# Two-layer transformer on one core: further expert blocks in pairs, pair adds on GpSimd, silu between the halves of the next weights

## Chip, cores, metric

One Trainium2 chip, one of its cores. The metric is the time of one execution on the device in microseconds. The kernel is one program that computes two transformer blocks; it is timed as a whole.

## What is computed

The first block is a mixer (differential attention and a state-space branch) and a mixture-of-experts feed-forward network; the second is a stack of two layers with banded and forgetting attention and a convolutional feed-forward network. All arithmetic is in float32. The change lies in the mixture of experts and in what follows it at once. There are 512 tokens of 1024 features; each goes to 8 of 64 experts with a hidden width of 256.

```python
def expert_block(args):            # one block: up to 128 rows of one expert
    tok_b, w_b, e = args
    xb = h[tok_b]
    hid = jax.nn.silu(xb @ w_e_gate[e]) * (xb @ w_e_up[e])
    return (hid @ w_e_down[e]) * w_b[:, None]

routed = segment_sum(out, buf_tok)           # 8 rows of each token added
shared = (silu(h @ w_sh_gate) * (h @ w_sh_up)) @ w_sh_down
f = routed + shared
x = x + gt2 * rmsnorm(f, g_post_ffn)         # then the next block's rms_norm(x)
```

An expert that has more than 128 tokens needs further blocks.

## The kernel before

**Engines and order.** The function `experts` runs one instruction list on each engine: SyncE (`sp`) asks for the weights, GpSimd (`pool`) gathers token rows from DRAM and scatters results with indirect DMAs, TensorE (`pe`) multiplies, ScalarE (`act`) and VectorE (`dve`) do the rest. Each engine works its list strictly in the order in which it is written; engines wait for each other by semaphores only.

**Main blocks.** The 64 main blocks, one per expert, are unrolled (`for n in range(N + 1)`, lines 3232, 3344 and 3507). Float32 products are made of three faster ones: each matrix is split in a rounded high part (ScalarE, a copy to `F32R`) and a low part (VectorE, value minus high part), and `three` multiplies high by high, high by low and low by high. For block n, ScalarE rounds the gate half and the up half of the weights (`round_gate_up`, L3303, two instructions of 128x2048), VectorE makes their low parts (`part_gate_up`, L3394). TensorE waits for both low parts (`gu_parted`, 2n + 2) and issues 24 matmuls (3 for each of 8 slices, each over 512 columns that hold gate and up together). Then ScalarE makes the silu (L3353) and VectorE the product with the up part (L3518), TensorE turns it (`turn_hid`, L3165), ScalarE and VectorE split it, and the 12 down matmuls follow one block later. TensorE's list per block is: gate and up of n, turn the gathered rows of n + 2 (`turn_x`, L3160), down of n - 1, turn hid of n. ScalarE's: split hid of n - 1, round gate and up of n + 1, silu of n, round down of n (L3309), round x of n + 2, evict y of n - 1 (L3362). VectorE's runs likewise. Weights lie in three sets of buffers (`SETS = 3`); those of block n are asked for when the gate and up matmuls of block n - 3 are done.

**Further blocks.** A loop with a trip count from the data (`Fori(0, n, 1)`, lines 3066, 3130, 3271, 3374, 3534) takes blocks beyond the 64, one after the other, with one set of buffers and plain float32 matmuls. In a round TensorE does gate and up, turns hid, does down, and turns the next gathered rows. The first weights are asked for after the up and the down matmuls of main block 61.

**Combine.** `combine_norm` loads the 8 expert rows of each token, tile by tile (4 tiles of 128 tokens), in two halves of 4 rows. TensorE sums the first half and the shared expert's output in PSUM (`add`), VectorE adds the second half in two steps (`half`, L3654 over 2048 elements and L3655 over 1024), then both (`total`, L3660). Square and root (ScalarE, GpSimd), scaling and residual (`finish`, L3664 and L3665), and the weighing of the row for the next norm (`weigh`, L652) follow, then TensorE turns the row and ScalarE and VectorE split it (`high_out`, `low_out`). ScalarE and VectorE also split the first weights of the next stage ahead of time (`high_ahead`, `low_ahead`, L253).

Of the kernel before, what the change touches and what calls it, by code (L numbers as in the profile page):

```python
# [11 lines left out]
P = 128  # L12
# [146 lines left out]
class SplitRing:  # L159
# [63 lines left out]
    def low_ahead(self, c, dve):  # L223
        self.low(c, dve)
        self.low_made = True
# [2658 lines left out]
def experts(c, s, h_dram, table, y_dram, acc, early):  # L2884
# [48 lines left out]
    nrow = carve([TABLE], parts=1)  # L2933
# [52 lines left out]
    fetch = c.sb(s, "fetch_rows", [P, 4], I32)  # L2986
    give = c.sb(s, "give_rows", [P, 4], I32)
# [21 lines left out]
    l_gu_in, l_down_in, l_fetch_in, l_give_in = (c.sem(f"later_{n}") for n in ("gate_up_in", "down_in", "fetch_in", "give_in"))  # L3009
    l_gathered, l_scattered = c.sem("later_gathered"), c.sem("later_scattered")  # L3010
    l_up_done, l_silud, l_gated, l_turned, l_copied, l_down_done = (c.sem(f"later_{n}") for n in ("up_done", "silued", "gated", "hid_turned", "hid_copied", "down_done"))
    l_x_turned, l_x_left, l_x_right, l_y_ready = (c.sem(f"later_{n}") for n in ("x_turned", "x_left", "x_right", "y_ready"))
    passed = c.sem("waits_passed")
    with ExitStack() as sb:
        block = sb.enter_context(nc.Block())

        def trips(eng):
            return eng.value_load(count[0:1, 0:1], min_val=1, max_val=MOST_LATER)

        lset = N % SETS  # L3020

        @block.sync
        def _(sp):
# [10 lines left out]
            def later_gate_up(e):  # L3034
                for v, w in enumerate((gate_w, up_w)):
                    sp.dma_start(gu[lset][:, v], w[bass.ds(e, 1)].rearrange("o (p k) n -> p (o k) n", p=P)).then_inc(l_gu_in, 16)

            def later_down(e):
                sp.dma_start(wd[lset], down_w[bass.ds(e, 1)].rearrange("o (k p) n -> p (o k) n", p=P)).then_inc(l_down_in, 16)

            def weights(b):
                return sp.value_load(erow[0:1, bass.ds(b, 1)], min_val=0, max_val=EXPERTS - 1)
# [18 lines left out]
            sp.wait_ge(up_done, N - SETS + 1)  # L3061
            sp.sem_inc(l_up_done, 1)
            sp.wait_ge(down_done, N - SETS + 1)
            sp.sem_inc(l_down_done, 1)
# [9 lines left out]
            sp.wait_ge(l_gu_in, 32 * n)  # L3074
            sp.sem_inc(passed, 1)
            sp.wait_ge(l_down_in, 16 * n)
            sp.sem_inc(passed, 1)

        @block.gpsimd
        def _(pool):  # L3080
# [12 lines left out]
            def later_gather():  # L3093
                nc.gpsimd.indirect_dma_start(xg[0][:], None, h_dram, bass.IndirectOffsetOnAxis(fetch[:, 0:1], 0),
                                             bounds_check=SEQ - 1, oob_is_err=False).then_inc(l_gathered, 16)
# [15 lines left out]
            rows(fetch, l_fetch_in, N)  # L3111
            rows(give, l_scattered, N)
            for j in range(N + 3):
# [4 lines left out]
                elif j == N - 2:  # L3118
                    pool.wait_ge(x_turned, j + 1)
                    pool.wait_ge(gathered[0], 16 * (j // 2 + 1))  # L3120
                    pool.wait_ge(l_fetch_in, 16)
                    later_gather()
                if j >= 3:
                    scatter(j - 3)
            pool.wait_ge(gathered[1], 16 * (N // 2))
            pool.wait_ge(l_gathered, 16)
            rows(fetch, l_fetch_in, N + 1)
            pool.wait_ge(listed, 1)
            n = trips(pool)
            with pool.Fori(0, n, 1) as i:  # L3130
                pool.wait_ge(l_fetch_in, 16 * i + 32)
                pool.wait_ge(l_x_turned, i + 1)
                pool.sem_inc(passed, 1)
                later_gather()
                pool.wait_ge(l_scattered, 16 * i + 16)
                rows(give, l_give_in, i + N)
                pool.wait_ge(l_give_in, 16 * i + 16)
                pool.wait_ge(l_y_ready, i + 2)
                pool.sem_inc(passed, 1)
                nc.gpsimd.indirect_dma_start(y_dram, bass.IndirectOffsetOnAxis(give[:, 2:3], 0), y[0][:], None,  # L3140
                                             bounds_check=SEQ * TOP_K - 1, oob_is_err=False).then_inc(l_scattered, 16)
                pool.wait_ge(l_gathered, 16 * i + 32)
                rows(fetch, l_fetch_in, i + (N + 2))
            for p in range(2):
                pool.wait_ge(scattered[p], 16 * (N // 2))
            pool.wait_ge(l_scattered, 16 * n + 16)
            pool.wait_ge(l_gathered, 16 * n + 16)
            pool.wait_ge(l_fetch_in, 16 * n + 32)
# [3 lines left out]
        def _(pe):  # L3152
# [110 lines left out]
            pe.wait_ge(l_gathered, 16)  # L3263
            turn_x(0).then_inc(l_x_turned, 1)
# [3 lines left out]
            pe.sem_inc(l_turned, 1)  # L3268
            pe.wait_ge(listed, 1)
            n = trips(pe)  # L3270
            with pe.Fori(0, n, 1) as i:
                pe.wait_ge(l_x_left, i + 1)
                pe.wait_ge(l_x_right, i + 1)
                pe.wait_ge(l_gu_in, 32 * i + 32)
# [18 lines left out]
        def _(act):  # L3293
# [455 lines left out]
```

## Time and profile before

| | us |
|---|---|
| median of 3 runs | 3199.24 (3198.63 to 3200.02) |
| the profiled execution's own time | 3197.57 |
| its span | 3195.9 |
| TensorE matmuls busy | 2930.6 (92% of the span) |
| VectorE busy | 1774.6 (56%) |
| ScalarE busy | 1414.9 (44%) |
| GpSimd busy | 533.1 (17%) |
| main expert blocks | about 1115 to 1750 |
| further blocks | about 1751 to 1790 |
| combine | 1796 to 1866 |

The span runs from the first to the last instruction; the time also has what lies around it. All times within the kernel are counted from the start of the span. Busy time of an engine is the time in which its instructions ran, waiting left out. A line of the timeline gives start and duration, then engine, source line, operation, what is written and what is read; in square brackets how long the engine stood idle before it, and what ended that.

### The profile page before, as it was taken

Reading aid. Unit: us, or ns where it says so; the run is one execution under the profiler, and the core shown is the slowest. Engines: PE = TensorE matmul, PEld = TensorE weight load, DVE = VectorE, ACT = ScalarE, POOL = GpSimd, SP = SyncE. Lnnn points to the kernel's source line nnn. Section 1 sums busy time; section 2 is a strip of 40 time slices with the busy share of each in tenths; the row PEclk is TensorE's granted clock in tenths of the full one; section 3 lists DMA queues with packets and bytes.
Section 4 is the critical chain, followed back from the end, with each engine's and each line's share of the span. In section 5 each row is a group of like instructions: output and inputs, shape, how many; then the busy total and the mean of one; then the engine's idle time right before and its main releaser. Section 6 shows DMA issues by size and latency. Waiting matters only on the chain. (4 is left out here: it accounts for less than half of the span.)

```text
span 3195.9 us, 36485 instructions
## 1 busy us (share of the span) xinstructions
PE 2930.6 (92%) x14410; PEld 2346.5 (73%) x14410; DVE 1774.6 (56%) x2033; ACT 1414.9 (44%) x1832; POOL 533.1 (17%) x702
## 2 busy tenths in 40 slices
PE   7978899898998799999999679889999998889998
PEld 4856788787886387777777358678887797678887
DVE  4447745436544498888887253455544327455543
ACT  3324525336223188888787123433323225333322
POOL 0005514124101522222222100000000104000000
PEclk9989999998999799999999889999999999999999
DMA  5210101022652399999997632123332301223331
GB/s 199 60 55 1 56 32 54 27 54 73 211 191 92 114 338 365 364 370 370 373 373 304 261 113 93 53 81 92 105 105 66 96 27 54 73 80 93 93 105 40
DMA packets 276890, 455.94 MB, mean 143 GB/s; under 512 B 24400, under 2 KB 206288, under 8 KB 257648
## 3 DMA queue, kind: packets, MB, share of 16 engines
q1 hardware_dynamic: 250560, 398.82, 36.0%
q0 software_dynamic: 26160, 54.79, 4.8%
q8 instruction: 115, 1.88, 0.3%
q14 instruction: 55, 0.45, 0.0%
HBM read 450.63 MB, written 39.08 MB: 153 GB/s over the span
## 5 line engine op out<-in xcount | busy, mean ns | idle before, releaser
L253 DVE TENSOR_TENSOR weight_part<-weights,weight_part 128x2048 fp32r<-128x2048 f32 (+1 forms) x65 | 148.1, 2279 | 161.2 <-ACT weight_part L242 161.2
L1037 ACT ACTIVATE up_room<-banks,tap_columns 128x512 f32<-128x512 f32 x88 | 68.6, 779 | 314.0 <-PE banks L298 314.0
L293 PE MATMUL banks<-hT_r,weight_part 128*128 128x512 f32 x496 | 200.9, 405 | 4.6 <-PEq L878 2.9
L242 ACT ACTIVATE weight_part<-weights 128x2048 fp32r<-128x2048 f32 (+1 forms) x65 | 121.7, 1872 | 175.8 <-PE banks L293 169.9
L1078 DVE SCALAR_TENSOR_TENSOR up_room<-banks,tap_columns,up_room 128x511 f32<-128x511 f32 x88 | 65.9, 749 | 238.7 <-ACT up_room L1037 238.7
L298 PE MATMUL banks<-hT_r,weight_part 128*128 128x512 f32 x496 | 196.3, 396 | 0.0
L703 POOL TENSOR_SCALAR branch_mean<-branch_mean 128x1 f32<-128x1 f32 x20 | 4.4, 222 | 1113.2 <-ACT up_room L697 747.3
L293 PE MATMUL banks<-hT_r,weight_part_o 128*128 128x512 f32 x432 | 174.3, 403 | 7.1 <-PEq L110 4.2
L253 DVE TENSOR_TENSOR weight_part_o<-weights,weight_part_o 128x2048 fp32r<-128x2048 f32 (+2 forms) x49 | 106.9, 2181 | 129.5 <-ACT weight_part_o L242 129.5
L298 PE MATMUL banks<-hT_r,weight_part_o 128*128 128x512 f32 x432 | 170.5, 395 | 0.0
L297 PE MATMUL banks<-h_low,weight_part 128*128 128x512 f32 x432 | 169.7, 393 | 0.0
L297 PE MATMUL banks<-h_low,weight_part_o 128*128 128x512 f32 x432 | 169.2, 392 | 0.0
L3085 POOL DMA_INDIRECT gathered<-h_tokens,block_rows x64 | 113.0, 1765 | 225.0 <-PE banks L3160 205.2
L3155 PE MATMUL banks<-weights_r,gatheredT_r 128*128 128x512 f32 x336 | 131.9, 393 | 0.0
L242 ACT ACTIVATE weight_part_o<-weights 128x2048 fp32r<-128x2048 f32 (+2 forms) x49 | 89.4, 1824 | 95.9 <-PE banks L293 91.3
L293 PEld LDWEIGHTS banks<-hT_r,weight_part 128*128 128x128 f32 x496 | 94.7, 191 | 26.7 <-issue 7.2
L2623 DVE TENSOR_REDUCE minus_maxima<-banks 128x2 f32<-128x1536 f32 x32 | 56.2, 1757 | 97.8 <-PE banks L2532 97.8
L298 PEld LDWEIGHTS banks<-hT_r,weight_part 128*128 128x128 f32 x496 | 94.1, 190 | 22.2
L3090 POOL DMA_INDIRECT expert_rows<-lent,block_rows x64 | 64.5, 1008 | 244.2 <-ACT lent L3362 234.7
L3154 PE MATMUL banks<-gate_up_high,gatheredT_r 128*128 128x512 f32 x256 | 104.3, 407 | 0.0
L3154 PE MATMUL banks<-h_tokens_r,gatheredT_r 128*128 128x512 f32 x256 | 103.0, 403 | 0.0
L3394 DVE TENSOR_TENSOR weights_r<-weights,h_tokens_r 128x2048 fp32r<-128x2048 f32 x42 | 95.5, 2292 | 12.2 <-ACT h_tokens_r L3303 11.8
(704 smaller groups left out, 8746.3 us busy)
## 6 DMA issues: line engine op xcount, KB each, us to landing
weights<-in_w_e_gate SPq DMA_DIRECT2D x44, 1024.0 KB, 16.0
weights<-in_w_e_up SPq DMA_DIRECT2D x44, 1024.0 KB, 18.6
hT<-in_w_e_down SPq DMA_DIRECT2D x44, 1024.0 KB, 18.9
weights<-in_w_up SPq DMA_DIRECT2D x88, 512.0 KB, 5.1
gate_up<-in_w_e_gate SPq DMA_DIRECT2D x22, 1024.0 KB, 15.4
gate_up<-in_w_e_up SPq DMA_DIRECT2D x22, 1024.0 KB, 18.4
down<-in_w_e_down SPq DMA_DIRECT2D x22, 1024.0 KB, 18.8
weights<-in_w_down SPq DMA_DIRECT2D x20, 1024.0 KB, 5.0
```

Of the source, the lines that this page charges most:

```text
L242: c.nc.scalar.activation(self.parts[n % 2][0][:, 0:z], self.raw[n % RAW_SLOTS][:, 0:z], ACT.Copy).then_inc(self.high_ready, 1)
L253: c.nc.vector.tensor_tensor(low[:, 0:z], self.raw[n % RAW_SLOTS][:, 0:z], high[:, 0:z].bitcast(F32), ALU.subtract).then_inc(self.low_ready, 1)
L293: ins = c.nc.tensor.matmul(out, lhs[0], rhs[0], start=start, stop=False)
L297: c.nc.tensor.matmul(out, lhs[0], rhs[1], start=False, stop=False)
L298: return c.nc.tensor.matmul(out, lhs[1], rhs[0], start=False, stop=stop)
L1037: nc.scalar.activation(a[:, f % 2, v], c.ps[:, 2 * (f % 4) + v], ACT.Identity, scale=conv[:, 2, ch:ch + 1], bias=bias[:, ch:ch + 1]).then_ ...
L1078: nc.vector.scalar_tensor_tensor(a[:, f % 2, v, 1:], c.ps[:, 2 * (f % 4) + v, 0:SEQ - 1], conv[:, 1, ch:ch + 1], a[:, f % 2, v, 1:], ALU.m ...
L3085: nc.gpsimd.indirect_dma_start(xg[n % 2][:], None, h_dram, bass.IndirectOffsetOnAxis(tab[:, n, 0:1], 0), bounds_check=SEQ - 1, oob_is_err= ...
L3090: nc.gpsimd.indirect_dma_start(y_dram, bass.IndirectOffsetOnAxis(tab[:, n, 2:3], 0), y[n % 2][:], None, bounds_check=SEQ * TOP_K - 1, oob_ ...
L3154: nc.tensor.matmul(out, lhs[0], rhs[0], start=start, stop=False)
L3155: nc.tensor.matmul(out, lhs[0], rhs[1], start=False, stop=False)
L3394: nc.vector.tensor_tensor(gu_low[i][:, v], gu[i][:, v], gu_high[n % 2][:, v].bitcast(F32), ALU.subtract).then_inc(gu_parted, 1)
```

## The change

In the main blocks silu and its product move between the two halves of the next block's rounding and low parts. The further blocks run two at a time, each with buffers and semaphores of its own; an odd count is rounded up, and the count is at least two. Their weights are asked for as soon as the set is free. In the combine, GpSimd does the first of the two adds of `half` for tiles 0 to 2 and the low part of the first weights, and `finish` and `weigh` stand earlier in the lists.

```diff
 # ScalarE, main blocks
                 if n + 1 < N:
-                    round_gate_up(n + 1)
+                    round_half(n + 1, 0)
                 if n < N:
                     act.wait_ge(up_done, n + 1)
+                    if N - SETS <= n < N - 1:
+                        act.sem_inc(l_up_done[n - N + SETS], 2)
                     ...
                     nc.scalar.activation(sl[n % 2][:], c.ps[:, n % 2, 0:EF], ACT.Silu).then_inc(silud, 1)
+                    if n + 1 < N:
+                        round_half(n + 1, 1)
                     round_down(n)
 # VectorE, main blocks
                 if n + 1 < N:
-                    part_gate_up(n + 1)
+                    part_half(n + 1, 0)
                 if n < N:
                     dve.wait_ge(silud, n + 1)
                     ...
                     nc.vector.tensor_tensor(hid[n % 2][:], sl[n % 2][:], c.ps[:, n % 2, EF:2 * EF], ALU.mult).then_inc(gated, 1)
+                    if n + 1 < N:
+                        part_half(n + 1, 1)
                     dve.wait_ge(d_rounded, n + 1)
 # SyncE, further blocks
-            with sp.Fori(0, n, 1) as i:
-                e = weights(i)
-                sp.wait_ge(l_up_done, i + 1)
-                later_gate_up(e)
-                sp.wait_ge(l_down_done, i + 1)
-                later_down(e)
+            with sp.Fori(0, n, 2) as i:
+                e = [weights(p, i + p) for p in range(2)]
+                for p in range(2):
+                    sp.wait_ge(l_up_done[p], i + 2)
+                    sp.sem_inc(passed, 1)
+                    later_gate_up(p, e[p])
+                for p in range(2):
+                    sp.wait_ge(l_down_done[p], i + 2)
+                    sp.sem_inc(passed, 1)
+                    later_down(p, e[p])
 # TensorE, further blocks (up(p, ks): gate and up matmuls; down(p): down matmuls)
+                def down(p):
+                    pe.wait_ge(l_copied[p], i + 4)
+                    pe.wait_ge(l_down_in[p], 8 * i + 16)
+                    pe.wait_ge(l_y_ready[1 - p], i + 2 + 2 * p)
+                    ...
+                        up(0, range(KD)).then_inc(l_up_done[0], 2)
+                up(1, range(0, 4))
+                pe.wait_ge(l_gated[0], i + 4)
+                pe.wait_ge(l_copied[1], i + 2)
+                turn_hid(0).then_inc(l_turned[0], 2)
+                up(1, range(4, KD)).then_inc(l_up_done[1], 2)
+                down(0)
+                pe.wait_ge(l_gated[1], i + 4)
+                pe.wait_ge(l_copied[0], i + 4)
+                turn_hid(1).then_inc(l_turned[1], 2)
+                down(1)
+                for p in range(2):
+                    pe.wait_ge(l_gathered[p], 8 * i + 32)
+                    pe.wait_ge(l_x_left[1 - p], i + 2 + 2 * p)
+                    pe.wait_ge(l_x_right[1 - p], i + 2 + 2 * p)
+                    turn_x(p).then_inc(l_x_turned[p], 2)
 # GpSimd: four row fetches instead of two ahead of the main blocks; loop over pairs likewise
-            rows(fetch, l_fetch_in, N)
-            rows(give, l_scattered, N)
+            for p in range(2):
+                rows(fetch[p], l_fetch_in[p], N + p)
+                rows(give[p], l_scattered[p], N + p)
 # VectorE, routing: the count
-            L(V.tensor_scalar(nrow[:, 2:3], nrow[:, 0:1], 1.0, None, ALU.max))
+            L(V.tensor_scalar(even[:, 0:TABLE // 2], iota[0:1, 0:TABLE:2], nrow[:, 0:1], None, ALU.is_lt))
+            L(V.tensor_reduce(nrow[:, 1:2], even[:, 0:TABLE // 2], AX, ALU.add))
+            L(V.tensor_scalar(nrow[:, 2:3], nrow[:, 1:2], 1.0, 2.0, ALU.max, ALU.mult))
 # Combine, ScalarE
             square(1)
+            turn.high_out(c, act, 0)
             square_x(1)
             square(2)
-            turn.high_out(c, act, 0)
+            turn.high_out(c, act, 1)
             square_x(2)
             square(3)
-            turn.high_out(c, act, 1)
             c.split.high_ahead(c, act)
+            turn.high_out(c, act, 2)
             square_x(3)
-            turn.high_out(c, act, 2)
             turn.high_out(c, act, 3)
 # Combine, GpSimd
-            for t in range(NT):
-                root(t)
-                rows.root(c, pool, t)
+            def pairs(t):
+                r = got[:, (2 * t + 1) % 4]
+                pool.wait_ge(landed[(2 * t + 1) % 4], 16 * (t // 2 + 1))
+                nc.gpsimd.tensor_tensor(r[:, 0:2], r[:, 0:2], r[:, 2:4], ALU.add).then_inc(paired, 1)
+
+            pairs(0)
+            root(0)
+            pairs(1)
+            rows.root(c, pool, 0)
+            root(1)
+            pairs(2)
+            rows.root(c, pool, 1)
+            root(2)
+            rows.root(c, pool, 2)
+            root(3)
+            rows.root(c, pool, 3)
+            c.split.low_ahead_on(c, pool)
 # Combine, VectorE (half(t) waits for the pair add, and adds both itself for tile 3 alone)
             half(0)
             total(0)
+            finish(0)
             half(1)
-            finish(0)
             total(1)
-            half(2)
             weigh(0)
             finish(1)
+            half(2)
             total(2)
             turn.low_out(c, dve, 0)
-            half(3)
             weigh(1)
             finish(2)
+            half(3)
             total(3)
             turn.low_out(c, dve, 1)
             weigh(2)
             finish(3)
             turn.low_out(c, dve, 2)
-            c.split.low_ahead(c, dve)
             weigh(3)
             turn.low_out(c, dve, 3)
```

## Rows read from the trace of the kernel before

**Rows 1.** Busy time by stretch: us, busy of each engine (records), clock, DMA share, GB/s.
```profile
1120.00:1740.00 620.00, 596.04 (x2870) 482.14 (x2870) 539.44 (x377) 505.22 (x437) 171.90 (x123) 1.00 0.94 362
1740.00:1796.00 56.00, 38.03 (x118) 20.51 (x116) 6.84 (x11) 9.14 (x12) 9.51 (x12) 0.91 0.37 135
```
**Rows 2.** Timeline of TensorE: last gate and up matmul of blocks 0 and 63.
```profile
1120.99 0.40 PE L3156 MATMUL banks<-gate_up_high,lent_r 128*128 128x512 f32 x1
...
1743.20 0.39 PE L3156 MATMUL banks<-h_tokens_r,lent_r 128*128 128x512 f32 x1
```
**Rows 3.** Timelines of TensorE, ScalarE and VectorE, blocks 59 and 60.
```profile
1697.86 0.48 PE L3154 MATMUL banks<-h_tokens_r,gatheredT_r 128*128 128x512 f32 x1
...
1703.22 0.39 PE L3156 MATMUL banks<-h_tokens_r,lent_r 128*128 128x512 f32 x1
...
1709.06 0.48 PE L3154 MATMUL banks<-gate_up_high,gatheredT_r 128*128 128x512 f32 x1
...
1714.50 0.39 PE L3156 MATMUL banks<-gate_up_high,lent_r 128*128 128x512 f32 x1
...
1704.23 1.92 ACT L3303 ACTIVATE gate_up_high<-gate_up 128x2048 fp32r<-128x2048 f32 x1 [0.93 <-DMA gate_up<-in_w_e_up]
1706.05 0.36 ACT L3353 ACTIVATE lent<-banks 128x256 f32<-128x256 f32 x1
...
1706.18 2.29 DVE L3394 TENSOR_TENSOR gate_up_r<-gate_up,gate_up_high 128x2048 fp32r<-128x2048 f32 x1 [0.55 <-ACT gate_up_high L3303]
1708.39 0.41 DVE L3518 TENSOR_TENSOR lent<-lent,banks 128x256 f32<-128x256 f32 x1
```
**Rows 4.** Timelines of ScalarE, VectorE and TensorE behind the last main block.
```profile
1743.63 0.38 ACT L3353 ACTIVATE lent<-banks 128x256 f32<-128x256 f32 x1 [4.75 <-PE banks L3156]
1743.91 1.90 ACT L3309 ACTIVATE shared_gated_r<-down 128x2048 fp32r<-128x2048 f32 x1
...
1748.06 0.42 DVE L3511 TENSOR_TENSOR lent_r<-banks,hiddenT_r 128x256 fp32r<-128x256 f32 x1
...
1748.53 0.50 PE L3154 MATMUL banks<-shared_gated_r,hiddenT_r 128*128 128x512 f32 x1 [1.94 <-DVE lent_r L3511]
```
**Rows 5.** Line 2962, loads of gate and up weights: issue to landing.
```profile
DMA to landing us min/median/max: 4.8/16.6/21.1
```
**Rows 6.** Timelines of TensorE and ScalarE, the two further blocks.
```profile
1754.45 5.80 PE L3277 MATMUL banks<-weights,gatheredT 128*128 128x512 f32 x9 [1.98 <-issue]
1759.65 3.60 PE L3277 MATMUL banks<-weights,gatheredT 128*128 128x512 f32 x8
...
1765.41 3.67 PE L3287 MATMUL banks<-hT,hiddenT 128*128 128x512 f32 x8 [0.70 <-DVE hiddenT L3540]
1768.92 1.04 PE L3160 MATMUL banks<-ident,gathered 128*128 128x128 f32 x8
...
1769.26 1.11 ACT L3381 ACTIVATE lent<-banks,give_rows 128x1024 f32<-128x1024 f32 x1 [5.50 <-PE banks L3287]
...
1786.95 1.11 ACT L3381 ACTIVATE lent<-banks,give_rows 128x1024 f32<-128x1024 f32 x1 [5.50 <-PE banks L3287]
```
**Rows 7.** Timeline of VectorE in the combine.
```profile
1829.39 2.29 DVE L3654 TENSOR_TENSOR expert_rows<-expert_rows 128x2048 f32<-128x2048 f32 x1 [2.65 <-DMA expert_rows<-expert_rows]
...
1860.68 1.27 DVE L652 SCALAR_TENSOR_TENSOR x_gained<-x_tok,rstd,norm_rows 128x1024 f32<-128x1024 f32 x1
```
**Rows 8.** Timelines of GpSimd and VectorE where both have work, earlier stages.
```profile
440.80 1.83 POOL L2406 TENSOR_TENSOR kT_r<-kT,x_tok_r 128x768 fp32r<-128x768 f32 x1
...
440.83 2.36 DVE L614 TENSOR_TENSOR kT<-gate_rows,rope 128x512 f32<-128x512 f32 x1
443.22 0.69 DVE L616 TENSOR_TENSOR kT<-kT,gate_rows 128x512 f32<-128x512 f32 x1
...
578.80 0.45 POOL L2496 TENSOR_TENSOR oT_low_r<-oT_low,oT_r 128x128 fp32r<-128x128 f32 x1
...
578.86 0.47 DVE L2618 TENSOR_SCALAR gate_rows<-gate_rows,sum_squares 128x128 f32<-128x128 f32 x1 [3.22 <-POOL sum_squares L2492]
```

More of the change, by code:

```diff
@@ L224, in low_ahead, with low_ahead_on @@
         self.low(c, dve)
+        self.low_made = True
+    def low_ahead_on(self, c, pool):
+        n = self.lows
+        self.lows += 1
+        pool.wait_ge(self.high_ready, n + 1)
+        z = self.sizes[n]
+        high, low = self.parts[n % 2]
+        c.nc.gpsimd.tensor_tensor(low[:, 0:z], self.raw[n % RAW_SLOTS][:, 0:z], high[:, 0:z].bitcast(F32), ALU.subtract).then_inc(self.low_ready, 1)
         self.low_made = True
@@ L2932, in experts @@
     desti = carve([NT, TOP_K], I32)
-    nrow = carve([TABLE], parts=1)
+    nrow, even = carve([TABLE], parts=1), carve([TABLE], parts=1)
     at = used[0]
@@ L2985, in experts @@
     tab = c.sb(s, "block_rows", [P, N, 4], I32)
-    fetch = c.sb(s, "fetch_rows", [P, 4], I32)
-    give = c.sb(s, "give_rows", [P, 4], I32)
+    fetch = two("fetch_rows", [P, 4], I32)
+    give = two("give_rows", [P, 4], I32)
     xg = two("gathered", [P, D])
@@ L3017, in trips @@
         def trips(eng):
-            return eng.value_load(count[0:1, 0:1], min_val=1, max_val=MOST_LATER)
-        lset = N % SETS
+            return eng.value_load(count[0:1, 0:1], min_val=2, max_val=MOST_LATER)
+        lset = [(N + p) % SETS for p in range(2)]
         @block.sync
@@ L3124, in _ @@
                     scatter(j - 3)
-            pool.wait_ge(gathered[1], 16 * (N // 2))
-            pool.wait_ge(l_gathered, 16)
-            rows(fetch, l_fetch_in, N + 1)
+            for p in range(2):
+                pool.wait_ge(l_gathered[p], 16)
+                rows(fetch[p], l_fetch_in[p], N + 2 + p)
             pool.wait_ge(listed, 1)
             n = trips(pool)
[L3130 to L3143, printed above, removed]
+            with pool.Fori(0, n, 2) as i:
+                for p in range(2):
+                    pool.wait_ge(l_fetch_in[p], 8 * i + 32)
+                    pool.wait_ge(l_x_turned[p], i + 2)
+                    pool.sem_inc(passed, 1)
+                    later_gather(p)
+                for p in range(2):
+                    pool.wait_ge(l_scattered[p], 8 * i + 16)
+                    rows(give[p], l_give_in[p], i + (N + p))
+                for p in range(2):
+                    pool.wait_ge(l_give_in[p], 8 * i + 16)
+                    pool.wait_ge(l_y_ready[p], i + 4)
+                    pool.sem_inc(passed, 1)
+                    nc.gpsimd.indirect_dma_start(y_dram, bass.IndirectOffsetOnAxis(give[p][:, 2:3], 0), y[p][:], None,
+                                                 bounds_check=SEQ * TOP_K - 1, oob_is_err=False).then_inc(l_scattered[p], 16)
+                    if p == 0:
+                        for q in range(2):
+                            pool.wait_ge(l_gathered[q], 8 * i + 32)
+                            rows(fetch[q], l_fetch_in[q], i + (N + 4 + q))
@@ L3262, in _ @@
             pe.wait_ge(x_parted, N)
-            pe.wait_ge(l_gathered, 16)
-            turn_x(0).then_inc(l_x_turned, 1)
+            for p in range(2):
+                pe.wait_ge(l_gathered[p], 16)
+                if p:
+                    pe.wait_ge(l_x_left[0], 2)
+                    pe.wait_ge(l_x_right[0], 2)
+                turn_x(p).then_inc(l_x_turned[p], 2)
             pe.wait_ge(gated, N)
@@ L3331, in _ @@
                     nc.scalar.activation(by_row[:, tile, b * 64:(b + 1) * 64], c.ps[:, TURNED_AT[tile] + b].rearrange("p (q r) -> p q r", r=KD), ACT.Copy).then_inc(copied, 1)
-            round_gate_up(0)
+            for v in range(2):
+                round_half(0, v)
             for f in range(2):
```

188 lines of the change are left out of this document (98 added, 90 removed).

## Prediction

> **What bounds the kernel now.** I read the table by slices first, then stretches of it, then the timeline of single blocks, the later blocks and the combine. The change touches one stretch, from 1,100 to 1,866 us; it adds nothing ahead of it that lies on a path, and behind it the same work follows, only sooner or later. So the question is how long three stages in it take.
>
> In the stage of the 64 main blocks [rows 1] four things are nearly full at once: TensorE is busy 596 of 620 us at the full clock, VectorE 539, ScalarE 505, and the DMA engines 94% of the time. The question is which of them sets the time of a block. The last gate and up matmul of block 0 starts at 1120.99 and that of block 63 at 1743.20 [rows 2]: 622.2 us for 63 steps, 9.88 us each. Call that moment of block n U(n).
>
> Block 59 shows what ends last [rows 3]. U(59) is 1703.22. The up half of block 60's weights lands a little late; ScalarE rounds it from 1704.23, and VectorE takes its low part from 1706.18 (1.95 us after the rounding began, 2.29 us long). The silu of block 59 stands in ScalarE's queue behind that rounding and starts at 1706.05, the product stands in VectorE's queue behind the low part and starts at 1708.39, TensorE can turn the product only then and starts block 60 at 1709.06: 5.84 us after U(59). Where the weights are in time the same step is about 4.0 us, all of it TensorE's own work (turning a gathered block, the down matmuls, turning hid). So a block costs 9.4 us where weights are early, up to 11 where they are late, 9.88 in the mean: transfers pace it, but TensorE's queue is only half a microsecond below.
>
> **The change in the main blocks.** It puts silu(n) ahead of the rounding of the second half of block n+1's weights, and the product ahead of that half's low part. No instruction is added. What it removes is the wait just seen, product and turning behind the late half. What it adds is a new dependence: both engines take their queues in order, so the second half of block n+1 cannot be rounded before silu(n), silu(n) not before U(n), and every gate and up matmul of block n+1 (they take both halves at once, line 3240, behind the wait on two more low parts) not before that half is done. Before, rounding and low part of block n+1 ran under the matmuls of block n. The cycle from U(n) to U(n+1), each link from a row:
> - U(n) to silu: 0.43 us (1743.20 to 1743.63) [rows 2, 4].
> - silu to the next ScalarE instruction when that one's data are there: 0.28 (1743.63 to 1743.91) [rows 4].
> - start of a rounding to start of its low part: 1.95 [rows 3].
> - low part 2.29 [rows 3], and 0.05 from VectorE's end to TensorE's start (1748.06 + 0.42 = 1748.48, start at 1748.53) [rows 4]: 2.34.
> - first to last of the 24 matmuls: 5.36 in block 59, 5.44 in block 60 [rows 3]; 5.40.
>
> The sum is 10.40 us. TensorE's own work between (about 4.0 of the 5.0 us from U(n) to the next start) hides in it. It is a floor for every one of the 63 steps, where before the mean was 9.88: 655.2 - 622.2 = **33.0 us lost**. Nothing else lengthens the cycle by my count. VectorE needs about 8.5 us and ScalarE about 8.2 of it. The weights of block n+2 are asked for at U(n-1) and take 16.6 us in the median, 21.1 at most [rows 5]; their second half is wanted only two cycles and 0.7 us after that, at 21.5, so even the slowest is in time, and 9.88 us worth of transfers fit into 10.40. Late transfers, which cost now, are then absorbed. If the steps of silu and rounding overlapped more than I see, 10.3 would give 27 us; if late weights came on top in the busiest blocks, 10.5 would give 39.
>
> **The further blocks.** There are two of them in this run (two rounds of the loop in the trace). Before, one took 17.69 us, from one eviction to the next (1769.26 to 1786.95) [rows 6], and TensorE idles while silu, product and copy of the same block pass. In its parts: gate and up, 16 records from 1754.45 to 1763.25, 8.80 us, since the clock is low at first (0.91 granted in the mean of the stretch [rows 1]); at the full clock a record takes 0.44 (the down matmuls: (3.67 - 0.59)/7), so 7.04. Down begins at 1765.41, and its eviction 3.85 later, 1.11 long. After, counted from the start of the first gate and up matmul: up(0) 8.80; up(1) 7.04 with the turning of hid(0), 0.4, between its halves, which hides silu and product of block 0; then down(0) from 16.2, its eviction from 20.1 to 21.2; down(1) waits for that eviction (same banks) and runs from 21.2, its eviction starts at 25.1. Before, the second eviction started 1786.95 - 1754.45 = 32.5 after. That is 7.4 saved. In front of it stands a second turning of gathered rows, 1.04 us [rows 6], which waits for the copy of the first (0.8): 1.9 lost. Weights of both are asked for at U(61) and U(62) and are there. Net **5.5 us gained**; the bounds are 3 (a stall when the second down starts, or a slower loop entry with more registers) and 8 (all clock back).
>
> **The combine.** Here VectorE's queue sets the time: it is full from tile 1 on, and the last weighing starts at 1860.68 [rows 7]. The change takes three adds of 2.29 us [rows 7] and the low part of the first weights, 2.28 for the same length, off VectorE and puts them on GpSimd, and moves finish and weighing forward. GpSimd's own adds: 1.83 us for 768 elements [rows 8]; by length 4.9 for 2048, a little less with a fixed part, so 4.75. If the engines ran side by side, VectorE would be rid of the adds of tiles 1 and 2 and of the low part: 2.29 + 2.29 + 2.28 = 6.9, some 7 us gained. The add of tile 0 gives nothing: GpSimd takes 2.5 us longer for it than VectorE did, most of which the wait for TensorE's sum of that tile hides.
>
> But they don't. GpSimd's subtract at 440.80 runs 1.83 us, and VectorE's add of 512 elements, which starts 0.03 later and has two operands in SBUF, takes 2.36 us instead of 0.69 [rows 8]: it stood until GpSimd was through. The 0.69 is L616's just behind it, of the same size and kind, when GpSimd is through. Now the places. The second rows of tile 2 land at 1829.39 [rows 7], a few tenths from the time at which the root of tile 1 lets finish(1) start (total of tile 1 near 1827, square and root 2.2 to 2.4 more): finish has two operands in SBUF, so it or its second half waits for the whole 4.75 us, which is 4.65 on the path to half(2). The low part on GpSimd follows the last root in its queue; the last weighing waits for that same root. Both get free together, and a GpSimd instruction that follows its own root starts first: 578.80 against VectorE's 578.86 behind the same root [rows 8]. So the weighing waits 4.65 more. 7 - 4.65 - 4.65 = -2.3, less about 0.8 that is won back in VectorE's idle time behind the first: **1.5 us lost** instead of 7 gained. Bounds: 7 gained when nothing collides, 6 lost when the small roots also wait each time behind VectorE's adds.
>
> The Trainium skill, page "SBUF — State Buffer", section "SBUF: two separate sides", says that VectorE and GpSimd share a port pair as an exclusive lock, taken for a whole instruction by a VectorE instruction with two SBUF inputs; by that rule, too, the combine gains nothing, and the trace agrees (2.36 us instead of 0.69). Its page "GPSIMD Engine Reference", section 3.1, gives 4.497 us for such an add of 2048 elements; the sum by it would be 0.8 us lower; no row of this kernel shows that size on GpSimd.
>
> Three more edits cost nothing. Two small VectorE instructions ahead of the block count (some 0.2 us each) lie in front of 8 us in which VectorE waits for ScalarE. Two more row fetches on GpSimd, 0.6 us each, end before the third gather's wait does. More semaphores are cleared between stages; at most a microsecond.
>
> **Sum.** 33.0 - 5.5 + 1.5 = +29.0 us. The profiled execution took 3197.57, so 3226.6; it lies 1.7 below the median of 3199.24, so **3228 us** in the median, 0.9% slower.
>
> **Rivals.**
> - *Adds run free.* The combine gains 7 instead of losing 1.5: 3219.7. Against it stands the collision in the rows; for it, that my places rest on times within a microsecond, and a different order could dodge one of the two. Chance 0.13.
> - *Transfers go on pacing the blocks, so the reorder costs nothing* (the other side). The DMA engines are 94% busy, and ScalarE's and VectorE's waits in this stage lead back to landings [rows 3]. If the period stayed 9.88, the sum would be 3199.2 - 5.5 + 1.5 = 3195.2. It decides if the cycle of five links is really under 9.9, that is, if rounding and low part of the second half took 0.5 us less than the rows say, or if the order on the queues did not bind. I see no way for either; removing the late product would then help too, some microseconds more. Chance 0.05 within 0.2%, 0.03 beyond it.
> - *The cycle is longer than its floor.* If late weights or a late low part of the down weights push the rounding back, say 10.65 per block, it is 16 us more: 3244. VectorE's last instruction before the next product ends only some 0.1 us ahead of it. Chance 0.07.
> - The forecast itself: 0.72.
>
> **Numbers.** About 0.2% (6.4 us) is what a measurement of this kernel can tell from none. Slower holds forecast, free adds and long cycle: 0.92. Same 0.05, faster 0.03. The range takes in 27 to 39 for the blocks and the combine's bounds, not the ends together: 3216 to 3238.
>
> **What the profile after would show.** Distances from U(n) to U(n+1) nearly constant at 10.4; TensorE idle some 0.7 us before each block, ended by VectorE's L3394 line, not by the product; ScalarE's waits for weights nearly gone and the DMA share down to about 0.9; product about 0.85 us after U(n) in all blocks. One pass of about 25 us from first gate and up matmul to last eviction. In the combine the adds on GpSimd 4.5 to 4.9 us, a finish instruction of some 5.9 us, and a last weighing of about 6. I am wrong if the distance is under 10.2, or if the last weighing is short.

## Result and the profile after

The changed kernel takes 3233.56 us in the median, against 3199.63 for the kernel before beside it: ratio 1.0102, 95% interval 1.0087 to 1.0116, 1% slower. The forecast was 3228 in 3216 to 3238. Its own executions scatter more than usual, 3225.78 to 3235.34; the profiled one is the fastest (span 3224.1, against 3195.9). A second measurement of the unaltered kernel (below) has its ratio at 1.0107 and a profiled span of 3232.0. One of the four executions of the reorder alone (10278 us) and one of the eleven of the pairs alone (11563 us), further below, took over three times as long as the rest and are left out of the medians given there.

I follow both traces by the same moments, with U(n) as in the prediction. "To the loads" runs from U(63) to the issue of the combine's first load, "combine" from there to the end of the last weighing.

| | before | after | after, second trace |
|---|---|---|---|
| U(0) | 1120.99 | 1120.69 | 1121.86 |
| U(0) to U(63) | 622.2 | 660.1 | 660.1 |
| to the loads | 52.39 | 45.00 | 45.02 |
| combine | 66.36 | 66.83 | 66.86 |
| all behind it | 1333.9 | 1331.5 | 1338.2 |
| span | 3195.9 | 3224.1 | 3232.0 |

The 28.2 us of the first pair of spans are +37.9 - 7.4 + 0.5, less 0.3 ahead and 2.4 behind. In the second trace the three changed stages agree to 0.03 us; the 8 us between the two lie ahead of block 0 (1.2) and behind the combine (6.7), in stages whose code is the same.

By stretches (columns as in [rows 1], whose lines these answer), the changed kernel:

```profile
1120.00:1779.00 659.00, 606.47 (x2875) 488.36 (x2874) 537.19 (x376) 499.47 (x438) 126.19 (x124) 0.99 0.91 346
1779.00:1832.00 53.00, 35.15 (x120) 20.27 (x118) 7.51 (x11) 9.86 (x13) 9.53 (x12) 0.89 0.30 109
1832.00:1900.00 68.00, 46.95 (x122) 23.73 (x123) 41.76 (x30) 17.36 (x26) 28.45 (x20) 0.81 0.77 296
```

The stage of the main blocks holds the same busy time of VectorE (537 for 539) and ScalarE (499 for 505) in 39 us more, and the DMA share has fallen from 0.94 to 0.91: neither does more, both wait more. TensorE's records add up to 606 us for 596, at nearly the same count (2875 for 2870). Where the engines wait stands in the timelines of TensorE, ScalarE and VectorE from U(59) to U(60), the step of [rows 3]:

```profile
1738.88 0.39 PE L3171 MATMUL banks<-h_tokens_r,lent_r 128*128 128x512 f32 x1
...
1743.92 0.47 PE L3169 MATMUL banks<-gate_up_high,gatheredT_r 128*128 128x512 f32 x1 [0.77 <-issue]
...
1749.30 0.39 PE L3171 MATMUL banks<-gate_up_high,lent_r 128*128 128x512 f32 x1
...
1739.31 0.38 ACT L3392 ACTIVATE lent<-banks 128x256 f32<-128x256 f32 x1 [2.45 <-PE banks L3171]
1739.59 1.91 ACT L3339 ACTIVATE gate_up_high<-gate_up 128x2048 fp32r<-128x2048 f32 x1
...
1739.72 0.42 DVE L3569 TENSOR_TENSOR lent<-lent,banks 128x256 f32<-128x256 f32 x1 [0.47 <-ACT lent L3392]
1741.53 2.29 DVE L3442 TENSOR_TENSOR gate_up_r<-gate_up,gate_up_high 128x2048 fp32r<-128x2048 f32 x1 [1.39 <-ACT gate_up_high L3339]
```

The chain is the one forecast. Silu starts 0.43 behind the last matmul, the rounding 0.28 behind it, the low part 1.94 behind that; it ends at 1743.82, TensorE starts at 1743.92, and its last matmul starts 5.38 later: 10.42 us. The waits say the same for the whole stage (engine, line, what it waited for: us in total, times, longest):

```profile
ACT lent L3392 <- PE banks L3171: 160.0, 63, 6.0
...
PE banks L3169 <- issue: 49.1, 62, 1.7
DVE lent L3569 <- ACT lent L3392: 34.4, 63, 3.0
DVE weights_r L3442 <- ACT h_tokens_r L3339: 29.1, 21, 1.5
DVE weights_r L3442 <- ACT gate_up_high L3339: 29.1, 21, 1.4
```

ScalarE now waits 63 times, once a block, for TensorE, 2.5 us each; no wait of it for weights is left. TensorE waits 62 times, 0.79 us each, and then starts at the end of a low part: the trace puts that down to "issue", because nothing but that semaphore stands in between. The distances from U(n) to U(n+1) are 10.41 at least and 10.43 in the median; the first alone is 12.97.

### The profile page after: what moved, and what is told of

It reads as the page before. It is cut to its first block and busy times, and to the rows that moved or that the text cites. A ratio compares the mean times of both kernels' runs of the same rounds, so it can differ in the third digit from the quotient of the medians.

```text
span 3224.1 us, 36567 instructions
## 1 busy us (share of the span) xinstructions
PE 2937.4 (91%) x14418; PEld 2349.6 (73%) x14418; DVE 1773.8 (55%) x2032; ACT 1409.0 (44%) x1833; POOL 511.3 (16%) x710
## 5 line engine op out<-in xcount | busy, mean ns | idle before, releaser
L3442 DVE TENSOR_TENSOR weights_r<-weights,gate_up_high 128x2048 fp32r<-128x2048 f32 x42 | 96.0, 2287 | 29.1 <-ACT gate_up_high L3339 29.1
L3093 POOL DMA_INDIRECT gathered<-h_tokens,block_rows x64 | 65.2, 1018 | 280.1 <-PE banks L3175 265.6
```

Source lines behind the costliest of these rows:

```text
L3093: nc.gpsimd.indirect_dma_start(xg[n % 2][:], None, h_dram, bass.IndirectOffsetOnAxis(tab[:, n, 0:1], 0), bounds_check=SEQ - 1, oob_is_err= ...
L3442: nc.vector.tensor_tensor(gu_low[i][:, v], gu[i][:, v], gu_high[n % 2][:, v].bitcast(F32), ALU.subtract).then_inc(gu_parted, 1)
```

## The experiments

**The three parts alone, and the whole again.** Only the main blocks' reorder, on the kernel before:

```diff
                 if n + 1 < N:
-                    round_gate_up(n + 1)
+                    round_half(n + 1, 0)
                 ...silu(n)
+                    if n + 1 < N:
+                        round_half(n + 1, 1)
                 # VectorE: part_half(n + 1, 0), product(n), part_half(n + 1, 1) likewise
```


> The kernel before with the reorder in the main blocks alone: silu(n) between the two roundings of block n+1, product between the two low parts. My theory (a cycle of five links, 10.44 us, in every one of the 63 steps): distances between the last gate and up matmuls constant at 10.4 us, main blocks some 35 to 38 us longer, 3235 to 3238 us. The rival (transfers pace the blocks whatever the order): distances spread from 9.4 to 11 with a mean of 9.9, 3200 us.

Measured 3237.83 against 3197.56, ratio 1.0128 (1.0110 to 1.0147). The blocks take 658.2 us, distances 10.38 to 10.52 with 10.44 in the median. One part alone makes the whole loss, and the distance is as good as constant.

Only the further blocks in pairs (the changed kernel with both halves ahead of the silu again and the combine of before):

> The kernel before with the further blocks in pairs, their buffers, semaphores, early loads and the even count, and nothing else. My theory: 7.4 us less between the last main block and the first load of the combine (the trace after shows 45.0 instead of 52.4), so 3192 us, main blocks 622 us as before. The rival (what they gain is given back, since the stage behind starts with a lower clock or its loads come later): 3197 to 3200.

Measured 3193.83 against 3197.56, ratio 0.9988 (0.9979 to 0.9997). Blocks 622.3; to the loads 43.45 instead of 52.39, so 8.9 us gained in this trace. The whole kernel gains less, 3.7 us by the medians and 1.0 to 6.7 by the interval. Part of this is the choice of the trace: with the further blocks untouched the stretch takes 49.6 to 52.4 us in seven traces (mean 51.3), and the kernel before has the longest; with the pairs it takes 43.4 to 45.0 in five (mean 44.1). So the stage gains about 7.2 in the mean. Behind it this trace is 0.4 longer in the combine and 1.9 after it than the kernel before. How much of the gain is given back there in the other executions stays open.

Only the combine:

> The kernel before with the new combine alone (pair adds of tiles 0 to 2 and the low part of the first weights on GpSimd, finish and weighing earlier). My theory (a VectorE instruction with two operands in SBUF stands while GpSimd's instruction runs, twice on the path): the last weighing takes about 5.4 us and ends within 1 us of before, 3199 to 3201 us. The rival (adds beside VectorE's work are free): last weighing 1.3 us, 7 us gained, 3193.

Measured 3198.98, ratio 1.0007 (0.9998 to 1.0016). Its combine takes 66.77 us, 0.4 more than before, which is within the scatter of the old combine (66.0 to 67.4 in seven traces); the last weighing is 5.41 long, as in the changed kernel.

The changed kernel unaltered:

> The changed kernel once more, unaltered. Three of its four executions took 3233 to 3235 us and the profiled one 3226, with a mean granted clock of 0.961 to 0.963 against 0.967. If the difference is in the granted clock of other stages, a second profile near 3233 us shows the main blocks at the same 10.4 us and lower clock in stretches outside the three changed stages; if it is in the changed stages, it shows there.

Measured 3231.93, ratio 1.0107 (1.0091 to 1.0122). In per cent the parts give 1.28 - 0.12 + 0.07 = 1.23, the whole 1.02 and 1.07; the intervals of the terms are wide enough for that.

**Which engine's order costs.** VectorE's product between its low parts, ScalarE's list as before:

```diff
                 # ScalarE: both halves rounded ahead of silu(n), as before
                 # VectorE
                 if n + 1 < N:
-                    part_gate_up(n + 1)
+                    part_half(n + 1, 0)
                 ...product(n)
+                    if n + 1 < N:
+                        part_half(n + 1, 1)
```


> The kernel before with half of the reorder: ScalarE rounds both halves of block n+1 and then makes silu(n), as before; VectorE makes the product between the two low parts. My theory: it is ScalarE's rounding behind the silu that closes the cycle. Without it, from the last gate and up matmul of a block: silu 0.43, product 0.81, low part 1.1 to 3.4, next block possible at 3.5, which is under TensorE's own 4.0; mean distance 9.9, 3199 to 3201 us. The rival (a low part behind the product is enough to lengthen the step): distance 10.1 or more, 3213 us or more.

Measured 3201.67 against 3199.04, ratio 1.0007 (0.9998 to 1.0017); blocks 622.8. The low part behind the product costs nothing while its rounding is not behind the silu.

And a shorter cycle: the same order, but three quarters of the weights are rounded and split ahead of silu and product, one quarter behind:

```diff
+    PIECES = ((0, slice(0, KD)), (1, slice(0, 4)), (1, slice(4, KD)))
-                    round_gate_up(n + 1)
+                    for q in range(2):
+                        round_piece(n + 1, q)
                 ...silu(n)
+                        round_piece(n + 1, 2)
                 # VectorE: part_piece likewise around the product
```


> The reorder with another size: three quarters of block n+1's gate and up weights are rounded and split ahead of silu and product, one quarter (1024 of 4096 columns) behind them. The kernel is otherwise the one before. My theory of five links: 0.43 + 0.28 + 1.0 + 1.2 + 0.05 + 5.4 = 8.4 us, under TensorE's 9.4, so the links bind no more and the distance is back at 9.8 to 9.95; 3198 to 3204 us. The rival (the reorder costs by more instructions or by the late silu itself, not by what stands behind it): over 3225 us.

Measured 3198.34, ratio 1.0000 (0.9990 to 1.0009); blocks 623.8, distances 8.57 to 11.87. With half the work in the rounding and the low part the cycle is some 2 us shorter, falls below the pace of the transfers, and no longer binds. The first step shows it directly, since TensorE has no down matmuls yet to fill it: 8.57 us here, 10.48 with the whole reorder.

The quarter does not gain either, but it removes less than the reorder does. The up half lands in one transfer, and a part of it is still rounded and split ahead of silu and product. ScalarE and VectorE where it landed late:

```profile
1553.62 1.06 ACT L3304 ACTIVATE h_tokens_r<-gate_up 128x1024 fp32r<-128x1024 f32 x1 [0.49 <-DMA gate_up<-in_w_e_up]
1554.58 0.37 ACT L3356 ACTIVATE lent<-banks 128x256 f32<-128x256 f32 x1
...
1553.15 3.43 DVE L3399 TENSOR_TENSOR gate_up_r<-gate_up,h_tokens_r 128x2048 fp32r<-128x2048 f32 x2 [0.24 <-ACT h_tokens_r L3304]
1556.50 0.42 DVE L3525 TENSOR_TENSOR lent<-lent,banks 128x256 f32<-128x256 f32 x1
```

Of the two, only the version with VectorE's order changed takes the product from behind the late half's low part, and its mean distance is still 9.9: that part of the wait was worth nothing. A silu ahead of the late half's rounding was run only with the cycle closed, so what it would be worth without the cycle is not shown.

**What the transfers cost in either order.** 192 KB more per block, copied from the down weights of the block to a buffer in DRAM that nothing reads, on the kernel before and on the reorder alone:

```diff
             for n in range(SETS, N):
                 gate_up(n)
+                sp.dma_start(spare[n], down_w[n][0:48]).then_inc(copied_out, 16)
```


> The kernel before, and with each of main blocks 3 to 63 a copy of 192 KB from DRAM to DRAM that nothing uses: 5 to 10% more transfers per block. If transfers pace its blocks, as I read the trace: distances longer by 0.4 to 0.9 us in the mean, 3225 to 3255 us. If they don't: within 5 us of before.

> The same copies added to the kernel with the reorder in the main blocks alone. My theory (its blocks wait for the cycle of five links at 10.44 us and transfers have 5% to spare): at most 10 us over that kernel, and 3235 to 3248 us, so that it stands within 10 us of the kernel before with the same copies. The rival (transfers and the cycle add): as much over it as the copies cost the kernel before.

In the old order 3225.46, ratio 1.0082 (1.0065 to 1.0098); blocks 646.0 instead of 622.2, distances 7.35 to 13.32. In the new order 3238.49, ratio 1.0121 (1.0104 to 1.0138), for 3237.83 with the reorder without copies. By the medians the same copies cost 26 us in the one order and none that can be told in the other. The traces say where. In the kernel before, 34 of the 63 steps take at most 9.55 us, the pace of TensorE's own work; the others are longer, mostly by late weights. With the copies only 16 are left at that pace. In the new order the blocks take 665.1 us with the copies and 658.2 without: 2.4 of these 6.9 are the first step (below), and 4.5 lie in ten steps of 10.6 to 11.4 us, all in the second half of the stage. So late transfers make the old order longer than TensorE's pace, and the new one has slack for most of them but not for all. That the two would come within 10 us of each other was a miss: they stay 13.0 apart. By stretches, 1120 to 1740 us of both, the old order with copies first:

```profile
1120.00:1740.00 620.00, 578.22 (x2771) 463.74 (x2770) 519.55 (x361) 485.01 (x420) 158.33 (x119) 1.00 0.96 372
```
```profile
1120.00:1740.00 620.00, 566.86 (x2690) 456.12 (x2688) 503.81 (x351) 470.22 (x408) 121.82 (x116) 0.99 0.94 361
```

The DMA share is 0.96 and 0.94, where [rows 1] has 0.94 without copies: in the old order the DMA engines had little room left.

**The collisions in the combine.** Both kernels have the further blocks in pairs and the new combine, the main blocks in the old order. In the first the low part of the first weights goes back to VectorE, behind the last weighing:

```diff
             rows.root(c, pool, 3)
-            c.split.low_ahead_on(c, pool)
             ...
             weigh(3)
+            c.split.low_ahead(c, dve)
             turn.low_out(c, dve, 3)
```


> Pairs of further blocks and the new combine, the main blocks in the order of before; and the low part of the first weights back on VectorE, behind the last weighing, where VectorE waits 1.9 us for the turned row. One of the two collisions is gone. My theory: last weighing 1.3 us instead of 5.4, the low part of 2.3 mostly in that hole, so the combine 3.5 us shorter than with the collision: 3199.5 - 7.4 + 0.5 - 3.5 = 3189. The rival (the weighing isn't what ends the stage): 3192.5.

Measured 3190.3 against 3199.88, ratio 0.9973 (0.9961 to 0.9985). Last weighing 1.28 us, combine 62.57: 4.2 less than with the new combine alone (66.77).

In the second tile 2's pair add is VectorE's as well:

```diff
             root(1)
-            pairs(2)
             rows.root(c, pool, 1)
             # VectorE, half(t): adds the pairs itself
-                if t == NT - 1:
+                if t >= 2:
```


> The same, and the pair add of tile 2 on VectorE too (as for tile 3), so that GpSimd adds only for tiles 0 and 1. Both collisions are gone. My theory: the finish instruction of tile 1 takes 1.2 us instead of 5.4, the add costs VectorE 2.3, so 2 us less than with one collision: 3187 us, the combine 5 us shorter than before. The rival (VectorE's load is what counts): no gain over the kernel with one collision, 3189 to 3191.

Measured 3189.33, ratio 0.9966 (0.9954 to 0.9978); combine 61.08. Its median is the lowest of all, 10.5 us below the kernel before beside it. From the version above it differs by less than the intervals; that the second collision was worth 1.5 us is read from the combine in the two traces. VectorE in its combine:

```profile
1822.76 1.23 DVE L3736 TENSOR_TENSOR x_tok<-x_tok,ffn_out 128x1024 f32<-128x1024 f32 x1
1823.90 2.29 DVE L3723 TENSOR_TENSOR expert_rows<-expert_rows 128x2048 f32<-128x2048 f32 x1
...
1847.24 1.29 DVE L661 SCALAR_TENSOR_TENSOR x_gained<-x_tok,rstd,norm_rows 128x1024 f32<-128x1024 f32 x1 [1.08 <-POOL rstd L645]
1848.44 2.29 DVE L262 TENSOR_TENSOR weight_part<-weights,weight_part 128x2048 fp32r<-128x2048 f32 x1
```

The finish of tile 1 is 1.23 long, though VectorE has one more add of 2.29 behind it, and the low part has moved behind the last weighing.

## Why the prediction was right, point by point

**Main blocks: forecast +33.0, measured +37.9.** The mechanism holds as written: a cycle over silu, rounding, low part and matmuls that was not closed before. Each link came within 0.05 us of its row, and their sum at the end of the stage is 10.42 for 10.40. The mean of the last 62 steps is (660.1 - 12.97)/62 = 10.44, so the floor was 0.04 short, which is 2.4 us over 63 steps. The other 2.5 is a term that I left out, the first step. In it TensorE runs the first 12 of block 1's 24 matmuls at the lower clock (granted 0.50 of full, 1.2 GHz), 0.63 us each where 0.39 is usual. This is the changed kernel's TensorE there:

```profile
1125.78 0.76 PE L3169 MATMUL banks<-h_tokens_r,gatheredT_r 128*128 128x512 f32 x1 [3.32 <-DVE weights_r L3442]
1126.34 0.63 PE L3170 MATMUL banks<-weights_r,gatheredT_r 128*128 128x512 f32 x1
```

Ahead of them it has idled for 3.32 us, because there is no block before block 0 whose down matmuls could fill the time. In the kernel before it idles 0.44 us between these two blocks, and the clock is full. The drop is not certain: with the reorder alone TensorE idled 3.33 us there too, kept the full clock, and the step took 10.48; with the extra copies it fell again (12.92). What decides it stays open. One reading of [rows 1] was a little off, and nothing rested on it: VectorE's and ScalarE's work per block come out as 8.6 and 8.1 us, not 8.5 and 8.2.

**The rival on the other side, transfers pace the blocks anyway, is out**, but its premise was right. Late transfers did make the old order longer than TensorE's own pace (the copies show it), and even so the reorder costs, because its cycle lies above that pace. That removing the late product "would then help too, some microseconds more" has no support: with the product taken from behind the late low part, and the cycle open, the blocks take 622.8 us for 622.2. In [rows 3] the low part itself ends at 1708.47, 0.59 us ahead of TensorE's start, so no more than that was to be had in such a block, by either engine's order. The rival of a longer cycle is out as well: in the changed kernel no step but the first is over 10.53. It takes more transfers than this kernel has to bring it in, as the ten long steps with the copies show.

**Further blocks: forecast -5.5, measured -7.4.** TensorE and ScalarE there:

```profile
1780.77 0.39 PE L3171 MATMUL banks<-h_tokens_r,lent_r 128*128 128x512 f32 x1
...
1794.37 10.54 PE L3294 MATMUL banks<-weights,gatheredT 128*128 128x512 f32 x24 [0.79 <-DVEq L3586]
...
1808.40 3.60 PE L3303 MATMUL banks<-hT,hiddenT 128*128 128x512 f32 x8
...
1813.45 3.67 PE L3303 MATMUL banks<-hT,hiddenT 128*128 128x512 f32 x8 [1.24 <-ACT lent L3429]
...
1801.66 0.38 ACT L3424 ACTIVATE lent<-banks 128x256 f32<-128x256 f32 x1 [7.38 <-PE banks L3294]
...
1812.19 1.11 ACT L3429 ACTIVATE lent<-banks,give_rows 128x1024 f32<-128x1024 f32 x1 [3.16 <-PE banks L3303]
1817.21 1.11 ACT L3429 ACTIVATE lent<-banks,give_rows 128x1024 f32<-128x1024 f32 x1 [3.90 <-PE banks L3303]
```

The order inside is as forecast, the second down waiting 1.24 us for the first eviction. Three sizes were off, and they partly cancel. The start lies 13.60 us behind U(63) instead of 11.25. Of these 2.35 us the second turning, costed at 1.9, has only 0.8: with the pairs but the old order in the main blocks the start lies 12.04 behind U(63), because the 1.98 us in which TensorE idled there [rows 6] take in most of it. The other 1.54 is the clock, which I had not counted: the down matmuls of block 63 take 4.44 us instead of 2.90, at 0.63 each:

```profile
1786.10 0.50 PE L3169 MATMUL banks<-shared_gated_r,hiddenT_r 128*128 128x512 f32 x1 [1.95 <-DVE lent_r L3562]
...
1786.73 0.63 PE L3171 MATMUL banks<-shared_gated_r,lent_r 128*128 128x512 f32 x1
...
1790.54 1.03 PE L3175 MATMUL banks<-ident,gathered 128*128 128x128 f32 x8
```

It is full again at 1790. TensorE idled 1.95 us ahead of them; in the kernel before it idled 1.94 at the same place [rows 4] and kept the full clock. And the last eviction starts 22.84 us behind the start, not 25.1, 2.3 better: I took the first gate and up at its 8.80 us of before, with the clock partly low; here 24 records take 10.54, 0.43 apart, so it is full from the first one. It is tempting to put this down to the shorter idle time ahead of them (0.79 us instead of 1.98), but the other runs speak against it. In four of the seven traces with the further blocks untouched, TensorE idles 1.95 to 1.98 us there as well and the clock is full from the first record, as in the reorder alone:

```profile
1791.53 7.11 PE L3277 MATMUL banks<-weights,gatheredT 128*128 128x512 f32 x16 [1.98 <-issue]
```

So 8.80 is one of two values that the old kernel itself takes, and 7.11 the other. In these four the whole stretch to the loads is 49.6 to 51.3 us instead of 52.39: 1.1 us or more of the gain measured here is the old kernel's own scatter. Net 32.5 - 22.84 - 2.35 = 7.3, and 0.1 between the last eviction and the loads. Without the fallen clock ahead, as in the run of the pairs alone, it is 8.9; against the mean of the seven traces it is 7.2 in the mean of the five with pairs.

**Combine: forecast +1.5, measured +0.5.** Both collisions are there, at the two places named. VectorE and GpSimd:

```profile
1859.51 1.28 DVE L3739 SCALAR_TENSOR_TENSOR ffn_out<-ffn_out,ffn_rstd,gate_rows 128x1024 f32<-128x1024 f32 x1 [0.99 <-POOL ffn_rstd L3700]
1860.83 5.43 DVE L3740 TENSOR_TENSOR x_tok<-x_tok,ffn_out 128x1024 f32<-128x1024 f32 x1
...
1887.19 5.41 DVE L661 SCALAR_TENSOR_TENSOR x_gained<-x_tok,rstd,norm_rows 128x1024 f32<-128x1024 f32 x1 [1.08 <-POOL rstd L645]
...
1850.23 4.51 POOL L3704 TENSOR_TENSOR expert_rows<-expert_rows 128x2048 f32<-128x2048 f32 x1 [2.56 <-DMA expert_rows<-expert_rows]
1854.83 1.26 POOL L643 TENSOR_SCALAR mean_square<-mean_square 128x1 f32<-128x1 f32 x1
...
1859.97 5.20 POOL L3704 TENSOR_TENSOR expert_rows<-expert_rows 128x2048 f32<-128x2048 f32 x1 [0.50 <-DMA expert_rows<-expert_rows]
...
1886.49 0.57 POOL L645 TENSOR_TENSOR rstd<-mean_square,minus_half 128x1 f32<-128x1 f32 x1
1887.02 4.50 POOL L233 TENSOR_TENSOR weight_part<-weights,weight_part 128x2048 fp32r<-128x2048 f32 x1
```

The second half of finish(1), two operands in SBUF, is issued 0.86 us behind GpSimd's add of tile 2 and takes 5.43 us instead of 1.23; it ends at 1866.26, 1.1 us after that add, about one duration of its own. The last weighing is issued 0.17 behind the low part and takes 5.41 instead of 1.28. They cost 4.20 and 4.13 us, where the forecast had 4.65 each: 0.97 less, about the whole difference. For the weighing, GpSimd's instruction took 4.50 us where I took 4.75, and VectorE came 0.17 behind it, not 0.1. For finish(1), VectorE came 0.86 behind, and GpSimd's add took 5.20, its first 0.82 us beside the first half of finish(1) (1859.51 + 1.28 = 1860.79). The +0.5 itself is no more than the scatter of the old combine, 66.0 to 67.4 us in seven traces; that nothing is gained is clear, that 0.5 is lost is not.

The Trainium skill gives 4.497 us for GpSimd's add (page "GPSIMD Engine Reference", section 3.1), and the trace agrees to 0.01 where VectorE is not in its way. The exclusive lock of the Trainium skill (page "SBUF — State Buffer", section "SBUF: two separate sides") is what the two rows of VectorE show. The prediction put the sum by the page's 4.497 at 0.8 us lower; the two waits that it shortens make that 0.5.

The experiments put a price on the collisions: without that of the weighing the combine is 4.2 us shorter, without that of finish(1) 1.5 more. The second is worth so little because VectorE has to make that add itself again, 2.29 us. **The rival that adds run free is out.** The best that was run is 66.36 - 61.08 = 5.3 us shorter, with two adds on GpSimd and the low part behind the last weighing.

**Total.** The terms' sum was +29.0. They measure 37.9 - 7.4 + 0.5 = +31.0, and the medians of the two kernels lie 33.9 apart. The remaining 2.9 are not located: the stages behind the combine, their code unchanged, take 2.4 us less in one trace of the changed kernel and 4.3 more in the other than in the one of before. That 3228 came out near is partly luck: the blocks' 4.9 us too few, and the further blocks' 1.9 and the combine's 1.0 too bad, offset each other.

## What to carry to other kernels

Before an instruction is moved between two halves of another block's work, write down the cycle that it closes: here silu(n) ahead of rounding(n + 1) turned a chain that ran one block ahead into one that starts at each block's last matmul. Add its links from the trace and compare the sum with the pace that something else already sets; above it each block pays the difference, and below it, at the one size tried, the move cost nothing and gained nothing. And give GpSimd long instructions only where VectorE has, for their whole length, nothing with two operands in SBUF on the path, least of all where both wait for the same instruction of GpSimd.

## What the hardware showed that I had not expected

- The collision goes both ways and reaches instructions of one element per partition: 1.26 us at 1854.83 instead of 0.22 for the scaling ahead of the root, which was issued 0.05 behind an add of VectorE with two operands in SBUF. GpSimd's add of tile 2, issued 0.46 us behind the first half of finish(1), took 5.20 instead of 4.51.
- GpSimd's gather instruction became cheaper though no edit touches it. Lines of the groups of GpSimd (busy time, mean ns of one, idle time before it and what ended it), before and then after:

```profile
L3085 POOL DMA_INDIRECT gathered<-h_tokens,block_rows x64 | 113.0, 1765 | 225.0 <-PE banks L3160 205.2 <-issue 14.4 <-DMA block_rows<-block_table 2.7
```
```profile
L3093 POOL DMA_INDIRECT gathered<-h_tokens,block_rows x64 | 65.2, 1018 | 280.1 <-PE banks L3175 265.6 <-issue 11.8 <-DMA block_rows<-block_table 2.7
```

  Its mean is 1018 ns instead of 1765. The trace of before shows why. In 50 of the 64 blocks VectorE is already in a low part of weights when the gather starts, an instruction of 2.29 us with two operands in SBUF, and the gather ends 0.86 to 0.94 us behind that instruction's end; in the other 14 it takes 0.99 to 1.06. One such pair:

```profile
1283.66 2.29 DVE L3394 TENSOR_TENSOR gate_up_r<-gate_up,gate_up_high 128x2048 fp32r<-128x2048 f32 x1 [0.35 <-ACT gate_up_high L3303]
...
1283.95 2.88 POOL L3085 DMA_INDIRECT gathered<-h_tokens,block_rows  x1 [3.23 <-PE banks L3160]
```

  VectorE ends at 1285.95 and the gather at 1286.83. In the new order the gather starts some 0.6 us ahead of the low part in nearly every block and takes 1.02. A VectorE instruction behind it is not held up there.
- Two executions of the changed kernel differ by 8 us while a stage of 660 us in them agrees to 0.03. The granted clock of that stage is 0.99 in both, the low stretch at its first step included. Behind 1900 us it is 0.98 and 0.97, and there TensorE is busy 1252.6 and 1261.4 us.
